# Joined prologue, five weight slots in the first projection, expert rows cleared in the first attention

## The reference

```
x    [1, 512, 1024]     tokens
mem  [1, 256, 1024]     memory rows, layer norm with gain mem_ln_g and shift mem_ln_b
memN = (mem - mean) * rsqrt(var + 1e-5) * mem_ln_g + mem_ln_b
k_mem, v_mem = memN @ w_mem_kv                        # 2 x 256 columns
q, k, v, q_mem = x @ na_w_in                          # 768, 768, 768, 256 columns
y = neighbourhood_attention(q, k, v, rpb), memory_attention(q_mem, k_mem, v_mem)
...
mod = silu(c_2) @ w_ada_2[0] + b_ada_2                # 6 x 1024 values, used in block 2
bias of block 2 = table rel_bias_2 by bucket of position differences
```

## Time and profile before

| | us |
|---|---|
| median of three runs | 3717.09 |
| the profiled execution | 3713.59 |
| its span | 3711.4 |
| first matmul of proj0 | at 44.48 |
| last matmul of proj0 ends | at 259.9 |
| first work of the stage na | at 265.9 |
| first load of the stage after na | at 333.4 |

### The profile page before, as it was taken

One profiled execution on the slowest core, in us unless ns is written; L12 is line 12 of the kernel. 1 busy time (PEld: TensorE's weight loads), 2 busy tenths in 40 slices (PEclk: granted clock), 3 DMA queues, 4 the chain that ended last, 5 costly groups with the idle time before them and its releaser, 6 DMA issues. The chain is left out here.

```text
span 3711.4 us, 42490 instructions
## 1 busy us (share of the span) xinstructions
PE 3224.1 (87%) x16212; PEld 1602.1 (43%) x16212; DVE 1310.1 (35%) x2927; ACT 666.1 (18%) x1382; POOL 381.3 (10%) x482
## 2 busy tenths in 40 slices
PE   6788599948978599909999999988789999999998
PEld 4445344423454344404444444475434443444344
DVE  5505211124062111152999961175421122212222
ACT  1115122221222122120010021154101010101011
POOL 1104111130002111131000000014100000000000
PEclk9889699978988699959999999999889999999999
DMA  6862399933001899625233443591679999999994
GB/s 222 259 218 91 142 360 354 350 117 99 1 1 58 285 367 358 253 91 185 102 126 112 125 171 114 189 352 58 242 281 422 407 407 406 422 406 406 405 418 203
DMA packets 282751, 889.54 MB, mean 240 GB/s; under 512 B 35761, under 2 KB 75009, under 8 KB 233489
## 3 DMA queue, kind: packets, MB, share of 16 engines
q1 hardware_dynamic: 250576, 798.11, 57.1%
q0 software_dynamic: 32064, 89.97, 6.7%
HBM read 806.97 MB, written 80.99 MB: 239 GB/s over the span
## 5 line engine op out<-in xcount | busy, mean ns | idle before, releaser
L2916 PE MATMUL ec_gu<-ec_ring,ec_xg 128*64 128x512 f32 x2048 | 454.6, 595 | 0.9 <-ACT ec_xg L3068 0.9
L231 PE MATMUL proj_ps<-xT,proj_w 128*128 128x512 f32 x992 | 433.3, 599 | 16.4 <-DMA proj_w<-in_na_w_in 16.4
L231 PE MATMUL proj_ps<-proj_w,xT 128*128 128x512 f32 (+2 forms) x896 | 360.0, 564 | 18.4 <-DMA proj_w<-in_w_in 18.4
L231 PEld LDWEIGHTS proj_ps<-xT,proj_w 128*128 128x128 f32 x992 | 190.3, 192 | 255.9 <-issue 238.1
L2916 PEld LDWEIGHTS ec_gu<-ec_ring,ec_xg 128*64 128x64 f32 x2048 | 142.0, 137 | 303.3 <-issue 303.3
L231 PEld LDWEIGHTS proj_ps<-proj_w,xT 128*128 128x128 f32 x896 | 172.1, 193 | 204.5 <-issue 155.8
L2945 PE MATMUL ec_yp<-ec_ring,ec_hT 128*64 128x512 f32 x1024 | 247.9, 635 | 0.0
L1152 PE MATMUL moe_gu_ps<-moe_w,moe_xg 128*64 128x512 f32 x1024 | 230.7, 604 | 17.7 <-ACT moe_xg L1267 17.7
L718 PE MATMUL mix_o<-mix_w,xT 128*128 128x512 f32 x384 | 172.2, 609 | 20.1 <-DMA mix_w<-in_w_out 20.1
L260 ACT ACTIVATE proj_o<-proj_ps 128x512 f32<-128x512 f32 (+1 forms) x120 | 70.8, 590 | 611.9 <-PE proj_ps L231 610.9
L2094 DVE SCALAR_TENSOR_TENSOR band_big<-proj_hit,proj_row,band_big 128x516 f32<-128x516 f32 x256 | 173.5, 750 | 2.4
(11 more groups left out here) (504 smaller groups left out, 3727.6 us busy)
## 6 DMA issues: line engine op xcount, KB each, us to landing
ec_ring<-in_w_gate SPq DMA_DIRECT2D x128, 1024.0 KB, 9.5
ec_ring<-in_w_up SPq DMA_DIRECT2D x128, 1024.0 KB, 11.8
ec_ring<-in_w_down SPq DMA_DIRECT2D x128, 1024.0 KB, 11.4
moe_w<-in_exp_w_gate SPq DMA_DIRECT2D x32, 2048.0 KB
moe_w<-in_exp_w_up SPq DMA_DIRECT2D x32, 2048.0 KB, 14.4
moe_w<-in_exp_w_down SPq DMA_DIRECT2D x32, 2048.0 KB, 10.9
proj_w<-in_w_in SPq DMA_DIRECT2D x22, 2048.0 KB, 10.9
proj_w<-in_w_ada SPq DMA_DIRECT2D x16, 1536.0 KB
```

The lines of the kernel that those rows point to most:

```text
L231: mm = nc.tensor.matmul(bank[0:jb["op"], 0:jb["ow"]], lhs, rhs, start=(k == 0), stop=(k == nk - 1))
L2916: mm = nc.tensor.matmul(gu_ps[n][half, :], xg[:, k, c0:c0 + CAP], w[:, m * D_FF + n * 512:m * D_FF + (n + 1) * 512], start=(k == 0), stop= ...
```

## The change

1. `consts`, `norm` of the memory, `turn_rows` and `condition` become one stage, `prologue`. SP issues the memory, x, `c_P`, gain and shift as 16 rows of 128 numbers (4 KB each instead of 512 KB) and then the weights of the first five chunks. PE turns x first, then gain and shift in one transpose, then the normalised memory. DVE makes the constants and the statistics before it waits for that transpose. DVE applies gain and shift as one operation per chunk of 128 columns, with a number per partition, while it copies from PSUM.
2. `proj0` has five weight slots instead of four. They belong to an object made before the prologue (`WeightSlots`) and freed after `proj0`, which costs one barrier more there.
3. The 20 clears of `slots` leave POOL and `proj0`. SP issues them in `na`, five behind each of the bias loads 2, 3, 4 and 5, and waits for all of them at its end.
4. `RelativeBias` sizes its work buffers by the groups that it makes. Unused helpers go.

The core of the diff:

```diff
+P0_SLOTS = 5
+class WeightSlots:
+    def load(self, sp, jb, j, r):
+        c0 = jb["col0"] + j * jb["cw"]
+        sp.dma_start(self.view(jb, r), jb["w"][:, :, c0:c0 + jb["cw"]]).then_inc(self.ready[r], 16)
+        if jb["add"] is not None:
+            sp.dma_start(self.add[r][:, 0:jb["cw"]], jb["add"][:, j * jb["cw"]:(j + 1) * jb["cw"]]).then_inc(self.ready[r], 16)
...
                 for m, n in enumerate(loads):
+                    if m < begun:
+                        continue
                     if m >= slots:
                         sp.wait_ge(bank_ready, first_tile[loads[m - slots] + 1])
+                    ws.load(sp, jb, j, slot[n])
...
-                if clear:
-                    nc.gpsimd.memset(z[:], 0.0).then_inc(z_ready, 1)
...
-                    more = len(zero_rows) * (n + 1) // len(chunks)
-                    for rows in zero_rows[rows_out:more]:
-                        pool.dma_start(rows, z[:]).then_inc(cleared, 16)
...
                     sp.dma_start(bias[m % NB][:], jb["bias_src"](p)).then_inc(b_in[m % NB], 16)
+                    if m == NB - 1 and zero_rows:
+                        sp.wait_ge(z_ready, 1)
+                    if m >= NB - 1:
+                        e = len(loads) - NB + 1
+                        for rows in zero_rows[len(zero_rows) * (m - NB + 1) // e:len(zero_rows) * (m - NB + 2) // e]:
+                            sp.dma_start(rows, z[:]).then_inc(cleared, 16)
+                if zero_rows:
+                    sp.wait_ge(cleared, 16 * len(zero_rows))
...
+def prologue(nc, a, x, xT, memT, condT, ident, strict, ones, iota, pidx, weights):
...
+            @block.sync
+            def _(sp):
+                for t in range(MT):
+                    sp.dma_start(m[:, t, :], a["mem"][0][t * P:(t + 1) * P, :]).then_inc(m_in[t], 16)
+                for t in range(NT):
+                    sp.dma_start(x[:, t, :], a["x"][0][t * P:(t + 1) * P, :]).then_inc(x_in[t], 16)
+                sp.dma_start(condT[:, :, 0], a["c_P"]).then_inc(c_in, 16)
+                sp.dma_start(rows[0:KD, :], a["mem_ln_g"].rearrange("(k p) -> k p", p=P)).then_inc(gb_in, 16)
+                sp.dma_start(rows[KD:2 * KD, :], a["mem_ln_b"].rearrange("(k p) -> k p", p=P)).then_inc(gb_in, 16)
+                weights(sp)
...
+            @block.tensor
+            def _(pe):
+                pe.wait_ge(id_ready, 1)
+                for n in range(2 * NT):
+                    t, c0 = n // 2, n % 2 * 4
+                    pe.wait_ge(x_in[t], 16)
+                    if n >= 4:
+                        pe.wait_ge(x_taken, n - 3)
+                    for c in range(4):
+                        mm = nc.tensor.transpose(xp[n % 4][:, c * P:(c + 1) * P], x[:, t, (c0 + c) * P:(c0 + c + 1) * P], ident[:])
+                    mm.then_inc(x_turned, 1)
+                pe.wait_ge(gb_in, 32)
+                nc.tensor.transpose(mp[0][:, 0:2 * KD], rows[:], ident[0:2 * KD, 0:2 * KD]).then_inc(gb_turned, 1)
+                pe.wait_ge(m_ready, 1)
+                for r in range(4):
+                    for c in range(2):
+                        for t in range(MT):
+                            f = (2 * r + c) * P
+                            mm = nc.tensor.transpose(mp[r][:, (2 * c + t) * P:(2 * c + t + 1) * P], m[:, t, f:f + P], ident[:])
+                    mm.then_inc(m_turned, 1)
...
+            @block.vector
+            def _(dve):
...
+                dve.wait_ge(gb_turned, 1)
+                V.tensor_copy(gb[:], mp[0][:, 0:2 * KD])
+                for t in range(MT):
+                    last = V.tensor_scalar(m[:, t, :], m[:, t, :], mv[:, t, 0:1], rstd[:, t:t + 1], ALU.subtract, ALU.mult)
+                last.then_inc(m_ready, 1)
+                for r in range(4):
+                    dve.wait_ge(m_turned, r + 1)
+                    for c in range(2):
+                        k = 2 * r + c
+                        V.tensor_scalar(memT[:, k, :], mp[r][:, c * N_MEM:(c + 1) * N_MEM], gb[:, k:k + 1], gb[:, KD + k:KD + k + 1],
+                                        ALU.mult, ALU.add)
+                dve.wait_ge(sig, 1)
+                V.tensor_mul(condT[:, :, 0], condT[:, :, 0], sg[:])
```

More of the change, by code:

```diff
@@ L300, in _ @@
                     last["finish"](pool)
-                if clear:
-                    pool.wait_ge(cleared, 16 * len(zero_rows))
             @block.vector
@@ new lines, in _ @@
+            @block.scalar
+            def _(act):
+                act.wait_ge(var_ready, 1)
+                nc.scalar.activation(sq[:], sq[:], ACT.Sqrt).then_inc(sqrt_ready, 1)
+                for n in range(2 * NT):
+                    t, c0 = n // 2, n % 2 * 4
+                    act.wait_ge(x_turned, n + 1)
+                    nc.scalar.activation(xT[:, c0:c0 + 4, t * P:(t + 1) * P], xp[n % 4][:].rearrange("p (c t) -> p c t", t=P),
+                                         ACT.Copy).then_inc(x_taken, 1)
+                act.wait_ge(c_in, 16)
+                nc.scalar.activation(sg[:], condT[:, :, 0], ACT.Sigmoid).then_inc(sig, 1)
@@ L417, in _ @@
[L417 to L428 removed]
+                V = nc.vector
@@ new lines, in _ @@
+                V.drain()
+                V.tensor_scalar(sq[:], mv[:, :, 1], LN_EPS, None, ALU.add).then_inc(var_ready, 1)
+                dve.wait_ge(sqrt_ready, 1)
+                V.reciprocal(rstd[:], sq[:])
+                V.drain()
+                dve.wait_ge(gb_turned, 1)
+                V.tensor_copy(gb[:], mp[0][:, 0:2 * KD])
+                for t in range(MT):
+                    last = V.tensor_scalar(m[:, t, :], m[:, t, :], mv[:, t, 0:1], rstd[:, t:t + 1], ALU.subtract, ALU.mult)
@@ L453, in pair_attention @@
     lo_hi = (slice(0, 64), slice(64, P))
+    zero_rows = [clear[b * P:(b + 1) * P, :] for b in range(clear.shape[0] // P)] if clear is not None else []
     with stage(nc, name) as st:
+        z = st.sb("z", [P, D]) if zero_rows else None
+        z_ready, cleared = st.sem("z_ready"), st.sem("cleared")
         bias = [st.sb(f"bias{r}", [P, 2, 1024]) for r in range(NB)] if loads else None
@@ L597, in _ @@
             def _(pool):
+                if zero_rows:
+                    nc.gpsimd.memset(z[:], 0.0).then_inc(z_ready, 1)
                 for s in range(N):
@@ L1391, in build @@
         cst = (ident, strict, ones, iota, pidx)
-        consts(nc, *cst)
         held = ctx.enter_context(ExitStack())
@@ L1450, in fetch_v @@
                     return dict(chunk=6, issue=issue, finish=lambda pool: pool.wait_ge(v_in, 16 * 2 * N_CB))
-                gemms(nc, "proj0", [mk_job, mv_job, v_job, k_job, q_job, mq_job, ada_job], order=order, slots=4,
-                      side=lambda st, evicted, first: RelativeBias(nc, a, biases, (2,), st), clear=(slots,), after=fetch_v)
+                gemms(nc, "proj0", [mk_job, mv_job, v_job, k_job, q_job, mq_job, ada_job], order=seq, slots=P0_SLOTS,
+                      side=lambda st, evicted, first: RelativeBias(nc, a, biases, (2,), st), after=fetch_v, held=ws, begun=P0_SLOTS)
+                nc.clear_and_free_semaphores(ws.ready)
+                nc.all_engine_barrier()
             by_rows = lambda v: v.rearrange("p (r b c) -> p b r c", r=ROWS, b=N_CB)
@@ L1985, in __init__ @@
         self.emptied = False
-        n, wd = sum(BIAS_WIDTH), max(BIAS_WIDTH)
+        n, wd = sum(BIAS_WIDTH), max(BIAS_WIDTH[g] for g in groups)
         self.pki, self.pk = st.sb("pki", [P, n], I32), st.sb("pk", [P, n])
```

275 lines of the change are left out of this document (56 added, 219 removed).

## The result

The changed kernel takes 3674.71 us (median of four runs, 3671.27 to 3677.59), the kernel before 3715.53 us on the same chip (four runs, 3709.97 to 3720.9). The ratio is 0.989, with a 95% interval of 0.9871 to 0.9908. The forecast was 3668 with a range of 3652 to 3686. A second set of runs of the changed kernel, at the end of the experiments, gave 3674.57 us and a ratio of 0.9876 (0.9857 to 0.9896). The profiled execution took 3671.27 us with a span of 3668.9.

A forecast was written before the change was run, and what follows sets the result against it. PE, busy 87% of the span, was taken as the bound, losing time before 266 us. Gains 22.9 + 23.9 + 2.2 + 0 = 49.0 us from 3713.6 give 3664.6, with 3.5 for the median 3668.1; range 3652 to 3686.

The forecast's parts named there:

- Part 1: Prologue: first matmul of proj0 at 21.6 us instead of 44.48, gain 22.9 us, with SP's blocked loads setting the barrier.
- Part 2: PE inside proj0: 191.5 us instead of 215.4, most waits for weights gone, one at k1 left.
- Part 3: End of proj0: 2.2 us less, POOL's drain falling from 4.47 to 1.86 us, an added barrier costing 0.4.
- Part 4: Clears in na: cost 0 us, loads up to b5 landed at about 302.3 before DVE wants it at 305.07.
- signs of being wrong: Prediction called wrong if k1's wait is far from 7 us, or if DVE waits for bias 5 in na.
- gain 25 if nothing holds SP: Bound on the prologue: proj0 starts at 19.5 us if SP's issues are not held.
- wait of 7 us at k1: In proj0: k1's weights land at 100.2 us, PE wants them at 92.9; 1.4 us of slow matmuls follow.
- cover of b5: In na: time between bias 5 landing and DVE wanting it, under 3 us.
- slower: Rival: clears on SP's queue do not overlap, 7.6 us each; net 36 us slower, 3753 us; chance 0.03.
- No wait at k1: Rival: v_na takes less of the SP queue in proj0; 8.4 us less, 3659.7 us; chance 0.22.
- the slots don't matter: Rival: waits at k1 and q1 come from DMA throughput alone; 25 us remain, 3692 us; chance 0.07.
- The wait grows: Rival: v_na passes whole, k1's wait is 13 us, ACT evictions hold PE's banks; 10 us more, 3678; chance 0.15.

The follow-up runs named there:

- three-load run: Changed kernel with three weight loads (mk, mv, v0) in the prologue instead of five, a0 and a1 issued in proj0; 3663.53 us in one run.
- shift run: Changed kernel with 64 more small transposes on PE at the end of the prologue; 3683.51 us in one run.
- run with the early drain: Changed kernel with one more GpSimd drain in both projections, in front of POOL's wait for the last chunk; 3683.59 us in one run.
- the one with the drain in the loop: Changed kernel with a GpSimd drain after every block of expert stores; 3662.48 us, ratio 0.9841.
- the one with all edits: Changed kernel with three loads, memory first, sigmoid ahead of most evictions, v_na by rows, both early drains, clears last; 3650.01 us, ratio 0.9796.

## Why the prediction was right, and where it was not

The time came out 7 us above the forecast and inside its range, and no part has the wrong sign. Parts 1 and 2 gave 20.6 and 20.0 us where 22.9 and 23.9 were forecast. Part 3 gave a third of its 2.2. In the second profile of the changed kernel part 2 gave only 15.4, so that the first came so near has some luck in it. One of the prediction's own signs of being wrong was met: DVE waited for bias 5 in na. Step by step:

- **Part 1, start at 21.6; measured 23.87.** The mechanism held: SP, blocked behind its own five loads, ends last. Both ends were priced too early, SP's by 1.9 us (22.80 for 20.9) and DVE's by 3.0 (21.65 for 18.7). SP's error is the DMA rate and the amount that stays out: at 20.9 us 6.8 MB had moved, not 7.2, and SP's last issue ended when 7.5 had, which leaves 2.5 MB out and not 2.8. DVE's error is the end of x: its last transposes ended at 15.3, not at 12.3 (at 13.5 in the second profile, where DVE ended at 19.8). The stage end took 1.07 us, not 0.7. The three-load run shows the blocking: without a0 and a1 in the prologue SP's last issue ends at 11.3, and the start moves by 3.85 us. The bound "gain 25 if nothing holds SP" fits that run, which gains 24.5; it was passed only where the queues of PE and ACT were reordered as well (27.9).
- **Part 2, 191.5; measured 195.4.** The slots remove the waits at k0, a7 and q1, and the run with four slots brings back those at a7 and q1 and one at k1; its proj0 is 11.1 us longer. The wait of 7 us at k1, which the prediction derived from v_na taking turns with the weights, isn't visible in the trace as such. In its place PE stands for 6.45 us on its instructions, and in this profile the weights arrive at the same moment, 104.0 us after the first matmul; the shift run shows the wait itself. So the size was right, and the reason is one of two that end together. The size has luck in it: the weights came 3.8 us later than the forecast 100.2, and without the stop in a7 PE would have wanted them some 4 us later than the forecast 92.9. In the second profile the weights came sooner, after 101.6 us, and the stop alone set k1. v_na is behind both: in all three runs that moved or cut it, the stop fell to 2.9 to 3.4 us, and PE waited for no weights at k1. The term that the sum lacked is the stop of 3.17 us in a4. The kernel before shows the same stop, 3.39 us in the a-chunks between v1 and k0, and the prediction, which read only waits with a releaser, passed it over. The rest is k0, at 22.37 instead of 20.87 behind that stop, less 0.6 at mk and 0.6 at k1 (6.45 + 1.33 where 8.4 were put): 3.2 + 1.5 - 0.6 - 0.6 = 3.5 of the 3.9.
- **Part 3, -2.2; measured -0.8.** The nearest row was the wrong one. The drain isn't the same for all stages without clears; it takes 0.082 us for each DMA that GpSimd issued, 20 clears are 1.6 us, and what was left are 34 others: v_na, nav, mod and the fill values. So it came to 2.84 us and not 1.86.
- **Part 4, 0; measured -0.5.** The clears overlap at 408 GB/s. The cover of b5, put at under 3 us, was used up: it landed at 263.26, 38.8 us behind the first load of na, where 36.4 were forecast (302.3 - 265.9). DVE waited 1.14 us, which the prediction had named as a sign of being wrong, and na didn't get longer by it. The rival "slower", with clears of 7.6 us one behind another, is refuted: all 20 and the biases went in 43.7 us. The fixed 2 us for each DMA of the Trainium skill (DMA: Bandwidth & Descriptors, "Anatomy of one DMA — SWDGE (gpsimd) path") are given there for GpSimd's path, and here SyncE issues. They don't add up in this queue, the trace says: 20 clears of 0.52 MB and six biases of 1.05 MB are 16.8 MB, which at 408 GB/s are 41 us by themselves, so nothing is left for 20 times 2 us.
- **The rivals.** "No wait at k1" and "the slots don't matter" are out by the runs named. "The wait grows" has the length of the second profile of the changed kernel: a stop of 7.82 us in a7 and 200.0 us for proj0. But not the mechanism, as k1's weights came sooner there; what came later were PE's instructions, behind the same v_na. How much of it falls on PE differs from run to run by some 4 us or more.

## What to carry to other kernels

Loads that are issued ahead of a barrier delay the barrier by the time that their issue is blocked: issue before it only what the next stage needs at once, and the rest right behind it. GpSimd pays for each of its DMAs once more at the end of a block, 0.08 us apiece on the path, unless it drains earlier beside other work; with the 96 DMAs of an expert layer one line is worth 7 us. And read the lines whose wait ends in "issue". The stops of PE that stood at no chunk's border belonged to the instruction stream and recurred at a fixed distance; DVE's wait at the border of a bias buffer had the same label and was a load.

## What the runs showed of the hardware

- **PE stops for its instructions when the DMA engines are full.** The stops lie 254 recorded matmuls or twice as many apart, move with the number of matmuls ahead of them, end 0.9 to 1.6 us after a packet of the instruction queue, and took 0.2 to 4.6 us in a4 or near it and 0.9 to 8.9 us in a7 or near it. The shortest are those of the shift run; without it, those of a7 took 5.8 to 8.9 us with v_na as it is and 2.9 to 3.4 with v_na moved or cut (3.6 with four slots, behind waits for weights). All of them stand among the short matmuls of the a-chunks, 64 in 1.50 us; packets of this queue that came in other places held nothing up.
- **Full DMA engines are not equally fast.** At a share of over 1.0 they moved 408 GB/s in na, 300 with v_na in loads of 96 KB, and 229 with v_na in loads of 384 KB.
- **The scatter of the long tail is the clock in the expert layers.** The seven periods of two expert blocks that can be read in a layer are 39.38 us each, or 41.07. Two neighbours in the changed kernel:

```profile
1381.04:1420.42 39.38, 37.20 (x330) 16.73 (x328) 5.54 (x12) 8.88 (x17) 6.09 (x12) 1.00 0.98 358
1420.42:1461.50 41.08, 38.90 (x331) 17.12 (x329) 5.54 (x12) 8.88 (x17) 6.09 (x12) 0.96 0.99 354
```

The work is the same and the granted clock 1.00 or 0.96, with a price of 1.7 us. The 0.96 is a mean. In the slow period one group of 16 matmuls holds the whole difference, and the pause before it is the same in both:

```profile
1407.96 3.65 PE L1166 MATMUL moe_y_ps<-moe_w,moe_hT 128*64 128x512 f32 x16 [0.74 <-DVEq L1222]
```
```profile
1447.34 5.35 PE L1166 MATMUL moe_y_ps<-moe_w,moe_hT 128*64 128x512 f32 x16 [0.74 <-DVEq L1222]
```

So the clock fell to 1.2 GHz for part of that group (the granted clock was 0.50 from 1450 to 1451 us), out of work in which PE was busy for 94% of the time. The changed kernel had 5 slow periods of 14 in its first profile and 3 in its second, the run with the early drain 12, the one with the drain in the loop 8, the one with all edits 6. That is 12 of the 16 us by which the tail of the early-drain run was longer than the changed kernel's, and 5 us between the last two runs. What decides how many there are stays open; no run was made for it.
